# Delta net: the squares of the output norm split into a rounded high part and a low part, summed by rounded products with ones

## The chip, the cores and the metric

The kernel runs on one core of one Trainium2 chip. The metric is the time of one execution on the device, in microseconds (us), as the median of several runs. A core has a matrix engine (TensorE, PE in the profile; its weight loads are PEld), an engine for elementwise work (VectorE, DVE), one for activation functions and copies (ScalarE, ACT), a general one (GpSimd, POOL) and an engine that issues transfers (SyncE, SP). They run side by side, each through its own list of instructions in order, and meet by semaphores. SBUF is the memory that all of them use; TensorE writes only to the eight banks of PSUM.

## The reference, cut to what matters

The program is a stack of layers over 256 tokens with 1024 features: gated feed-forward blocks, an mLSTM mixer, a gated delta net, and attention in a sliding window. All products are of f32 data. The change touches the end of the delta net, the RMS norm of its output over the 128 features of each of 16 heads:

```python
def rmsnorm_2(x, w):
    xf = x.astype(jnp.float32)
    y = xf * lax.rsqrt(jnp.mean(xf * xf, axis=-1, keepdims=True) + EPS)
    return (y * w.astype(jnp.float32)).astype(x.dtype)
...
    o = chunked_gated_delta_rule(q, k, v, g, beta)
    z = z.reshape(bsz, t, GDN_V_HEADS, GDN_HEAD_DIM).astype(jnp.float32)
    o = rmsnorm_2(o, out_norm_w) * jax.nn.silu(z)
    return o.reshape(bsz, t, GDN_V_DIM).astype(hn.dtype) @ w_out
```

## The kernel before, in words

Features lie on the 128 partitions and tokens along the free axis. Every large projection is made of products in a rounded f32 format (`F32R`, fp32r in the profile): a weight tile and an activation are each split into a rounded high part and the rest (`wh`, `wl`, `XH`, `XL`), and three products (high by high, low by high, high by low) are added up in PSUM. ScalarE makes the high parts of the weights (`hi`, L474) and VectorE or GpSimd the low parts (`lo`, L479), from tiles that SyncE brings in through four slots.

The delta net is one large class, `GCore`, in which each engine has its own order written out by hand. A list of step names stands for every engine (`self.A` ScalarE, `self.V` VectorE, `self.T` TensorE, `self.G` GpSimd), and a step's place in its list is the count of a semaphore: `past("sqr0")` waits for the step `sqr0`. Weight products of the projections are set between the steps of the recurrence (`d(h0, h1)` runs quarters of units, each quarter two tiles, that is six products).

The recurrence goes over four groups g = 0 to 3 of four heads, two chunks of 128 tokens each. For a group, TensorE transposes the values of the first chunk (`p1`) and the keys, applies the solved triangle (`p2`), transposes the second chunk (`p1b`), builds the state (`p3`), the first chunk's output (`p3b`), the state's part in the second chunk (`p4`), and the second chunk's values (`p5`) and output (`p6`). VectorE evicts `p1` and `p1b` with a factor (`e1`, L2631; `e1b`, L2645), the keys (`kd`, L2638) and `p4` (`e4`, L2655). ScalarE evicts the others (`e2`, `e3`, `e3b`, `e5` and, last, `e6`, L2263). The output o of a group of heads is then in `dVT`, 128x1024.

The norm is made group by group. `sqr` (ScalarE, L2267) writes the squares of o to `gRO`. `p7` (TensorE, L3277) multiplies them with a 128x128 tile of ones, two f32 products of 512 columns, so that every partition of the two banks holds the sum over the 128 features. `rl` (ScalarE, L2272) takes Ln of the mean, `re` (L2278) Exp of minus half of it. On VectorE `yz` (L2663) multiplies o by the gate, `yo` (L2669) by the norm, and after ScalarE's rounded copy `yh` (L2282) `yl` (L2673) forms the low part `YL`. The output projection `gout0` takes `YH` and `YL`, two of its units to a group; TensorE's unit 4 waits for `yl2`, unit 6 for `yl3`.

The functions that compute this, and the class's list of steps:

Of the kernel before, what the change touches and what calls it, by code (L numbers as in the profile page):

```python
# [23 lines left out]
F32 = mybir.dt.float32  # L24
# [5 lines left out]
P = 128  # L30
# [124 lines left out]
def program(nc, a):  # L155
    with ExitStack() as ctx:
# [1823 lines left out]
        def state_set(n, at, vb_at):  # L1980

            s, = carve(at, 2048, **{f"gS{n}": t4})
            y0, y1 = carve(at + (2176 if n == 0 else 2048), 4096, **{f"gY0_{n}": t4, f"gY1_{n}": t4})
            ro, = carve(at + (2176 if n == 0 else 2048), 4096, **{f"gRO{n}": ([P, HG, SEQ], F32)})
            vb0, vb1, kd = carve(vb_at, 6144, **{f"gVB0_{n}": t4, f"gVB1_{n}": t4, f"gKD{n}": t4})
            return s, y0, y1, ro, vb0, vb1, kd

        sets = [state_set(0, gw, gw + 21504), state_set(1, q0, q0 + 6144), state_set(2, ext + 16384, ext + 16384 + 6144)]
        S0, Y0, Y1, RO, VB0, VB1, KD = ([sets[n][i] for n in (0, 1, 2, 0)] for i in range(7))
        HOP = ((2, 3), (4, 5), (6, 7), (2, 3))  # L1990
        GB = (2, 3, 4, 2)
        KC, EGC, NB, NBC, NC, BW, B2, BR, RK = carve(
# [1 line left out]
            gNBC=([P, GDN_V, 2], F32), gNC=([P, 2, GDN_V], F32), gBW=([P, B], F32), gB2=([P, 2, GDN_V], F32),  # L1994
            gBR=([P, 2, GDN_V], F32), gRK=([P, GDN_V], F32))
        never = cst[:, C_NEVER:C_NEVER + P]
        WS, WS64 = (WS0, WS1), (WL0, WL1)
        BLOCKS = 4
        WP = [bank[2 + i][:, :].rearrange("p (j i) -> p j i", j=16) for i in (0, 1)]
# [5 lines left out]
        class GCore:  # L2005
# [5 lines left out]
            def __init__(self, gate, norm):  # L2011
                self.gate, self.norm = gate, norm
                self.A = steps("act", "gdn_act", (
# [7 lines left out]
                    " re3 yh3").split())  # L2021
                self.V = steps("dve", "gdn_dve", (
# [13 lines left out]
                    " tap43_0 yl0 e4_2 e1_3 kd3 yz1 yo1 yl1 e1b_3 e4_3 yz2 yo2 yz3 yl2 yo3 yl3").split())  # L2036
                self.T = steps("pe", "gdn_pe", (
# [3 lines left out]
                    " p1k_3 p5_2 p7_1 p2_3 p6_2 p1b_3 p3_3 p7_2 p4_3 p3b_3 p5_3 p6_3 p7_3").split())  # L2041
                self.G = steps("pool", "gdn_pool", (
                    "xzero xinit col em1 em0 em2 em3 br nb uzero tzero").split())
                self.s_wd, self.s_w, self.s_xd, self.s_tu = (sem(f"dma_g{n}") for n in ("wd", "w", "xd", "tu"))
                self.units = ([(gqk0, 0, j) for j in range(4)] + [(gk1, 0, j) for j in range(4)]
                              + [(gz1, 0, j) for j in range(4)] + [(gqk1, j // 4, j % 4) for j in range(8)]
                              + [(gz, j // 4, j % 4) for j in range(8)] + [(gv, j // 4, j % 4) for j in range(16)]
                              + [(gout0, 0, j) for j in range(8)] + [(gout1, 0, j) for j in range(4)])
                self.banks = ([4, 5, 6, 7, 1, 2, 3, 0] + [(1, 6, 7, 0)[j % 4] for j in range(8, WIDE)]
                              + [(1, 0)[j % 2] for j in range(WIDE, 44)])  # L2050
# [46 lines left out]
            def act(self, eng):  # L2097
# [166 lines left out]

                def sqr(g):
                    eng.wait_ge(*A.past(f"e6_{g}"))
                    A.done(eng.activation(RO[g][:, :, :], dVT[:, 4 * g:4 * g + 4, :], ACT.Square), f"sqr{g}")  # L2267

                def rl(g):
                    eng.wait_ge(*T.past(f"p7_{g}"))  # L2270
# [209 lines left out]
            def dve(self, eng):  # L2480
# [162 lines left out]
                def e1b(g):  # L2643
                    eng.wait_ge(*T.past(f"p1b_{g}"))
                    V.done(eng.tensor_tensor(VB1[g][:, :, :], quad(bank[HOP[g][0]][:, :], HG), beta(g, 1), ALU.mult),  # L2645
                           f"e1b_{g}")

                def e4(g):
                    eng.wait_ge(*T.past(f"p4_{g}"))
                    r = VB1[g]  # L2650
                    if g == 0:
                        eng.wait_ge(*G.past("nb"))
                    eng.wait_ge(*V.past(f"e1b_{g}"))
                    for h in four:
                        ins = eng.scalar_tensor_tensor(r[:, h, :], bank[HOP[g][1]][:, h * P:(h + 1) * P],  # L2655
                                                       NB[:, 4 * g + h:4 * g + h + 1], r[:, h, :], ALU.mult, ALU.add)
                    V.done(ins, f"e4_{g}")

                def yz(g):
                    o = dVT[:, 4 * g:4 * g + 4, :]  # L2660
                    eng.wait_ge(*A.past(f"sqr{g}"))
                    eng.wait_ge(*A.past(f"zs{g}"))
                    V.done(eng.tensor_tensor(o, o, Z[:, 4 * g:4 * g + 4, :], ALU.mult), f"yz{g}")  # L2663
# [126 lines left out]
                taps(42)  # L2790
                e1b(2)
                e1b(1)
                yz(0)
                yo(0)
                e4(1)
                taps(43)
                yl(0)
                e4(2)
                e1(3)
                kd(3)  # L2800
                yz(1)
                yo(1)
                yl(1)
                e1b(3)
                e4(3)
                yz(2)
                yo(2)
                lo(50)
                yz(3)
                yl(2)  # L2810
                yo(3)
# [240 lines left out]
            def pe(self, eng):  # L3052
# [221 lines left out]
                def p7(g):  # L3274
                    eng.wait_ge(*A.past(f"sqr{g}"))
                    for i in two:
                        mm = eng.matmul(bank[HOP[g][i]][:, :], ones[:, :],  # L3277
                                        RO[g][:, 2 * i:2 * i + 2, :].rearrange("p h t -> p (h t)"), start=True, stop=True)
                    T.done(mm, f"p7_{g}")

                gg()
# [1029 lines left out]
```

## Time and profile before

| | |
|---|---|
| median of 3 runs | 1259.97 us (1258.79 to 1260.63) |
| profiled execution | 1258.97 us, its span 1257.2 us |
| TensorE busy | 1239.2 us, 99% of the span |
| VectorE, ScalarE, GpSimd busy | 888.0, 762.9, 279.2 us (71%, 61%, 22%) |
| mean granted TensorE clock | 0.998 |

The span is the time from the first to the last instruction of the profiled execution. TensorE's busy time counts its matmuls, which overlap in a pipeline: the duration of a matmul in a row is longer than the slot it takes, and the slot is read as the distance from one start to the next. A row of the timeline merges equal instructions that follow each other (x4). "Idle before" in brackets is the time in which the engine had nothing running before the row, and the arrow names what ended it.

### The profile page before, as it was taken

The page shows a single profiled execution, that of the slowest core. Times are in us where ns is not written, and L with a number is a line of the kernel's source. Part 1 is how long each engine was busy: PE and PEld are TensorE (multiplying, and loading weights), DVE is VectorE, ACT ScalarE, POOL GpSimd, SP SyncE. Part 2 cuts the span into 40 slices and gives each one's busy share as a digit, 9 for nine tenths or more (in the row PEclk, how much of TensorE's full clock was granted, in tenths as well). Part 3 has the DMA queues.
Part 4 walks back from the last instruction along what each step waited for, and adds up shares of the span by engine and source line. Part 5 has one row for each costly group of instructions (what it writes and reads, how often), then busy time and mean ns, then how long its engine had stood idle before and what let it go on. Part 6 is the DMA issues. An engine that isn't in the chain of part 4 may idle for free.

```text
span 1257.2 us, 28670 instructions
## 1 busy us (share of the span) xinstructions
PE 1239.2 (99%) x10528; PEld 1213.8 (97%) x10528; DVE 888.0 (71%) x1627; ACT 762.9 (61%) x1284; POOL 279.2 (22%) x240
## 2 busy tenths in 40 slices
PE   9999999999999999999999999999999999999997
PEld 9999999998999999999999989999999989999997
DVE  6766556887787765587796557777766797877654
ACT  6544444598564445468876676666665576766642
POOL 0000000010000000028875320344530131444400
PEclk9999999999999999999999999999999999999999
DMA  7655465464356656646647134865577525665473
GB/s 248 203 170 176 138 173 180 146 193 133 103 175 203 186 155 186 209 131 217 187 155 207 56 102 144 226 196 185 162 204 205 168 69 168 185 190 184 134 205 104
DMA packets 89164, 212.53 MB, mean 169 GB/s; under 512 B 19509, under 2 KB 35701, under 8 KB 88960
## 3 DMA queue, kind: packets, MB, share of 16 engines
q1 hardware_dynamic: 86608, 204.32, 52.6%
q0 software_dynamic: 1632, 6.46, 2.1%
q8 instruction: 49, 0.80, 0.3%
q10 hardware_dynamic: 848, 0.72, 0.2%
q14 instruction: 27, 0.22, 0.1%
HBM read 208.41 MB, written 3.06 MB: 168 GB/s over the span
## 4 chain that ended last, share of the span: by engine, by line
PE 92%; DVE 4%; ACT 2%; issue 1%; DVEq 0%; ACTq 0%
PE bank L624 21%; PE bank L626 21%; PE bank L625 21%; PE bank L3077 3%; PE bank L3078 3%; PE bank L3079 3%; PE bank L1725 1%; PE bank L3212 1%; PE bank L1727 1%; PE bank L1726 1%; DVE wl L479 1%; PE bank L3730 1%; PE bank L3732 1%; PE bank L3731 1%; PE bank L583 1%
## 5 line engine op out<-in xcount | busy, mean ns | idle before, releaser
L474 ACT ACTIVATE wh<-raw 128x1024 fp32r<-128x1024 f32 (+2 forms) x418 | 402.0, 969 | 333.3 <-PE bank L626 288.8
L479 DVE TENSOR_TENSOR wl<-raw,wh 128x1024 fp32r<-128x1024 f32 (+3 forms) x348 | 380.4, 1097 | 139.8 <-ACT wh L474 139.0
L624 PE MATMUL bank<-XH,wh 128*128 128x256 f32 (+1 forms) x1432 | 406.5, 284 | 1.3 <-DVE XL L1064 1.2
L626 PE MATMUL bank<-XH,wl 128*128 128x256 f32 (+1 forms) x1432 | 405.9, 283 | 0.0
L625 PE MATMUL bank<-XL,wh 128*128 128x256 f32 (+1 forms) x1432 | 405.6, 283 | 0.0
L624 PEld LDWEIGHTS bank<-XH,wh 128*128 128x128 f32 x1432 | 270.6, 189 | 2.2 <-DVE XL L1064 1.4
L626 PEld LDWEIGHTS bank<-XH,wl 128*128 128x128 f32 x1432 | 271.0, 189 | 0.0
L625 PEld LDWEIGHTS bank<-XL,wh 128*128 128x128 f32 x1432 | 269.5, 188 | 0.0
L479 POOL TENSOR_TENSOR wl<-raw,wh 128x1024 fp32r<-128x1024 f32 x70 | 168.9, 2421 | 268.0 <-ACT wh L474 267.8
L624 PE MATMUL bank<-AH,wh 128*128 128x256 f32 (+1 forms) x704 | 198.9, 283 | 0.0
L626 PE MATMUL bank<-AH,wl 128*128 128x256 f32 (+1 forms) x704 | 198.7, 282 | 0.0
L625 PE MATMUL bank<-AL,wh 128*128 128x256 f32 (+1 forms) x704 | 198.4, 282 | 0.0
L625 PEld LDWEIGHTS bank<-AL,wh 128*128 128x128 f32 x704 | 132.9, 189 | 0.0
L626 PEld LDWEIGHTS bank<-AH,wl 128*128 128x128 f32 x704 | 132.4, 188 | 0.0
L624 PEld LDWEIGHTS bank<-AH,wh 128*128 128x128 f32 x704 | 132.2, 188 | 0.2
L3077 PE MATMUL bank<-gXH,wh 128*128 128x256 f32 x256 | 75.4, 295 | 0.0
L3078 PE MATMUL bank<-gXL,wh 128*128 128x256 f32 x256 | 71.7, 280 | 0.0
L3079 PE MATMUL bank<-gXH,wl 128*128 128x256 f32 x256 | 71.6, 280 | 0.0
L936 DVE TENSOR_TENSOR tp<-bank,R 128x256 f32<-128x256 f32 x88 | 37.3, 423 | 40.3 <-PE bank L626 33.1
L900 POOL TENSOR_TENSOR AL<-pr,AH 128x256 f32 (+1 forms) x44 | 36.4, 827 | 100.4 <-ACT AH L893 100.2
L948 ACT ACTIVATE bank<-tp,vec 128x256 f32<-128x256 f32 x88 | 48.8, 554 | 3.5 <-DVE tp L936 3.5
L3077 PEld LDWEIGHTS bank<-gXH,wh 128*128 128x128 f32 x256 | 48.2, 188 | 1.4 <-issue 1.0
(401 smaller groups left out, 2274.6 us busy)
## 6 DMA issues: line engine op xcount, KB each, us to landing
raw<-in_w_up SPq DMA_DIRECT2D x170, 512.0 KB, 4.4
raw<-in_w_down SPq DMA_DIRECT2D x64, 384.0 KB, 3.4
raw<-in_w_down SPq DMA_DIRECT2D x64, 320.0 KB, 3.2
raw<-in_w_gvz SPq DMA_DIRECT2D x32, 512.0 KB, 4.5
raw<-in_w_gout SPq DMA_DIRECT2D x16, 512.0 KB, 4.6
raw<-in_w_gqk SPq DMA_DIRECT2D x12, 512.0 KB, 4.0
raw<-in_w_mv SPq DMA_DIRECT2D x8, 512.0 KB, 4.6
raw<-in_w_mqk SPq DMA_DIRECT2D x8, 512.0 KB, 5.0
```

What stands on the lines that cost most here:

```text
L474: eng.activation(WH[s][:, 0:n, :], raw[s][:, 0:n, :], ACT.Copy).then_inc(s_hi[s], 1)
L479: eng.tensor_tensor(WL[s][:, 0:n, :], raw[s][:, 0:n, :], WH[s][:, 0:n, :].bitcast(F32), ALU.subtract).then_inc(s_lo[s], 1)
L583: mm = eng.matmul(bank[st.wide[g]][:, 0:T], WH[u][:, 2 * g + j, :], xl, start=False, stop=k == DC - 1)
L624: eng.matmul(out, WH[s][:, i, :], xh, start=start, stop=False)
L625: eng.matmul(out, WH[s][:, i, :], xl, start=False, stop=False)
L626: mm = eng.matmul(out, WL[s][:, i, :], xh, start=False, stop=stop)
L900: self.lows.done(eng.tensor_tensor(AL[:, bass.ds(j, 1), 0:T], PR[b][:, 0:T].unsqueeze(1), AH[:, bass.ds(j, 1), 0:T].bitcast(F32), ALU.subt ...
L936: leave(st, it, u, eng.tensor_tensor(TP[u % 2][:, 3:3 + T], bank[st.banks[u]][:, 0:T], R[:, 0:T], ALU.mult))
L948: self.tap2s.done(eng.activation(self.sums(u), TP[u % 2][:, 3:3 + T], ACT.Identity, bias=v(self.bias, m), scale=v(self.w, m + 88)), f"tap2 ...
L3077: eng.matmul(out, WH[s][:, i, :], xh, start=first, stop=False)
L3078: eng.matmul(out, WH[s][:, i, :], xl, start=False, stop=False)
L3079: mm = eng.matmul(out, WL[s][:, i, :], xh, start=False, stop=last)
```

## The change

The squares are computed twice. `sqr` on ScalarE now writes them in the rounded format, to a new tile `gROH` that lies over the group's `VB0` and `VB1`. VectorE gets a step `ro`, which forms the same squares in f32 in `gRO`, and `rol`, which takes `gROH` from them and writes the rest, in the rounded format, to `gROL`, in the same place as `gRO`. `p7` then has four products of 512 columns with the same tile of ones, read in the rounded format: two of `gROH`, a wait for `rol`, and two of `gROL` that add to the same banks.

```diff
@@ state_set @@
+            rol, = carve(at + (2176 if n == 0 else 2048), 4096, **{f"gROL{n}": ([P, HG, SEQ], F32R)})
+            roh, = carve(vb_at, 4096, **{f"gROH{n}": ([P, HG, SEQ], F32R)})
+            return s, y0, y1, ro, vb0, vb1, kd, roh, rol
...
+        onesr = ones[:, :].bitcast(F32R)
@@ GCore, ScalarE @@
                 def sqr(g):
                     eng.wait_ge(*A.past(f"e6_{g}"))
-                    A.done(eng.activation(RO[g][:, :, :], dVT[:, 4 * g:4 * g + 4, :], ACT.Square), f"sqr{g}")
+                    A.done(eng.activation(ROH[g][:, :, :], dVT[:, 4 * g:4 * g + 4, :], ACT.Square), f"sqr{g}")
@@ GCore, VectorE @@
+                def ro(g):
+                    o = dVT[:, 4 * g:4 * g + 4, :]
+                    eng.wait_ge(*A.past(f"e6_{g}"))
+                    V.done(eng.tensor_tensor(RO[g][:, :, :], o, o, ALU.mult), f"ro{g}")
+                    eng.wait_ge(*V.past(f"ro{g}"))
+                    eng.wait_ge(*A.past(f"sqr{g}"))
+                    V.done(eng.tensor_tensor(ROL[g][:, :, :], RO[g][:, :, :], ROH[g][:, :, :].bitcast(F32), ALU.subtract),
+                           f"rol{g}")
@@ the order on VectorE @@
                 e1b(1)
+                ro(0)
                 yz(0)
...
                 e4(2)
+                ro(1)
                 e1(3)
...
                 e1b(3)
+                ro(2)
                 e4(3)
                 yz(2)
                 yo(2)
                 lo(50)
+                ro(3)
                 yz(3)
@@ GCore, TensorE @@
                 def p7(g):
                     eng.wait_ge(*A.past(f"sqr{g}"))
                     for i in two:
-                        mm = eng.matmul(bank[HOP[g][i]][:, :], ones[:, :],
-                                        RO[g][:, 2 * i:2 * i + 2, :].rearrange("p h t -> p (h t)"), start=True, stop=True)
+                        eng.matmul(bank[HOP[g][i]][:, :], onesr[:, :],
+                                   ROH[g][:, 2 * i:2 * i + 2, :].rearrange("p h t -> p (h t)"), start=True, stop=False)
+                    eng.wait_ge(*V.past(f"rol{g}"))
+                    for i in two:
+                        mm = eng.matmul(bank[HOP[g][i]][:, :], onesr[:, :],
+                                        ROL[g][:, 2 * i:2 * i + 2, :].rearrange("p h t -> p (h t)"), start=False, stop=True)
                     T.done(mm, f"p7_{g}")
```

The names of the four steps `ro0 rol0` to `ro3 rol3` are set into VectorE's list in the same places. TensorE's and ScalarE's lists stay as they are.

In VectorE's order around group 0, before (`gVB1` is the eviction `e1b`, `dZ` the gate in `yz`, `gNB` the factor in `e4`):

```order
L2645 TENSOR_TENSOR gVB1_2_176<-bank6,gBR_185 128x512 [waits pe_gdn_pe]
L2645 TENSOR_TENSOR gVB1_1_169<-bank4,gBR_185 128x512 [waits pe_gdn_pe]
L2663 TENSOR_TENSOR dVT_97<-dVT_97,dZ_96 128x1024 [waits act_gdn_act]
L2669 SCALAR_TENSOR_TENSOR dVT_97<-dVT_97,vec_62,gRO0_160 128x1024 [waits dve_gdn_dve,act_gdn_act]
L2655 SCALAR_TENSOR_TENSOR gVB1_1_169<-bank5,gNB_180,gVB1_1_169 128x128 [waits dve_gdn_dve,pe_gdn_pe]
```

and with the change:

```order
L2649 TENSOR_TENSOR gVB1_2_180<-bank6,gBR_191 128x512 [waits pe_gdn_pe]
L2649 TENSOR_TENSOR gVB1_1_171<-bank4,gBR_191 128x512 [waits pe_gdn_pe]
L2666 TENSOR_TENSOR gRO0_160<-dVT_97 128x1024 [waits act_gdn_act]
L2669 TENSOR_TENSOR gROL0_164<-gRO0_160,gROH0_165 128x1024 [waits act_gdn_act,dve_gdn_dve]
L2676 TENSOR_TENSOR dVT_97<-dVT_97,dZ_96 128x1024 [waits act_gdn_act]
L2682 SCALAR_TENSOR_TENSOR dVT_97<-dVT_97,vec_62,gRO0_160 128x1024 [waits dve_gdn_dve,act_gdn_act]
L2659 SCALAR_TENSOR_TENSOR gVB1_1_171<-bank5,gNB_186,gVB1_1_171 128x128 [waits dve_gdn_dve,pe_gdn_pe]
```

The two new steps stand behind both evictions and ahead of `yz0`, `yo0` and `e4_1`.

In VectorE's order around groups 2 and 3, with the change (`YL` is `yl1`, then the eviction `e1b_3`; `wl2` is the weight split `lo50`; the last row is `yl2`):

```order
L2686 TENSOR_TENSOR YL_98<-dVT_97,YH_99 128x1024 [waits act_gdn_act]
L2649 TENSOR_TENSOR gVB1_0_162<-bank2,gBR_191 128x512 [waits pe_gdn_pe]
L2666 TENSOR_TENSOR gRO2_178<-dVT_97 128x1024 [waits act_gdn_act]
L2669 TENSOR_TENSOR gROL2_182<-gRO2_178,gROH2_183 128x1024 [waits act_gdn_act,dve_gdn_dve]
L2659 SCALAR_TENSOR_TENSOR gVB1_0_162<-bank3,gNB_186,gVB1_0_162 128x128 [waits dve_gdn_dve,pe_gdn_pe]
...
L479 TENSOR_TENSOR wl2_60<-raw2_52,wh2_56 128x1024 [waits s_hi2]
L2666 TENSOR_TENSOR gRO0_160<-dVT_97 128x1024 [waits act_gdn_act]
L2669 TENSOR_TENSOR gROL0_164<-gRO0_160,gROH0_165 128x1024 [waits act_gdn_act,dve_gdn_dve]
L2676 TENSOR_TENSOR dVT_97<-dVT_97,dZ_96 128x1024 [waits act_gdn_act]
L2686 TENSOR_TENSOR YL_98<-dVT_97,YH_99 128x1024 [waits act_gdn_act]
```

Before, these rows are the same without those of L2666 and L2669: `e4_3` follows `e1b_3`, and `yz3` follows the split.

In TensorE's order at `p7` of group 0, with the change:

```order
L3234 MATMUL bank6<-cst_63,dVT_97 128x128 x3
L3294 MATMUL bank2<-gROH0_165,ones_64 128x512 [waits act_gdn_act]
L3294 MATMUL bank3<-gROH0_165,ones_64 128x512
L3298 MATMUL bank2<-gROL0_164,ones_64 128x512 [waits dve_gdn_dve]
L3298 MATMUL bank3<-gROL0_164,ones_64 128x512
L3272 MATMUL bank5<-gS1_166,dQK_95 128x256 [waits act_gdn_act]
L3272 MATMUL bank5<-gS1_166,dQK_95 128x256
```

Before, two products of `gRO0` stand in the place of the four; the transpose ahead (`p1b` of group 2) and `p4` of group 1 behind are where they were. The wait for VectorE now stands between the second and the third.

## Rows read from the trace of the kernel before

**Rows 1.** The page, busy time by engine and the chain that ended last
```profile
PE 1239.2 (99%) x10528; PEld 1213.8 (97%) x10528; DVE 888.0 (71%) x1627; ACT 762.9 (61%) x1284; POOL 279.2 (22%) x240
...
PE 92%; DVE 4%; ACT 2%; issue 1%; DVEq 0%; ACTq 0%
```

**Rows 2.** Waits of TensorE: us in total, times, longest us
```profile
PE bank L3277 <- ACT gRO L2267: 0.4, 1, 0.4
```

**Rows 3.** Timeline of TensorE, 715 to 754 us: start us, us, what, [idle before]
```profile
715.51 0.60 PE L3217 MATMUL bank<-cst,dVT 128*128 128x128 f32 x4
715.95 1.88 PE L3277 MATMUL bank<-gRO,ones 128*128 128x512 f32 x4
717.67 1.03 PE L3255 MATMUL bank<-gS,dQK 128*128 128x256 f32 x4
...
730.16 1.88 PE L3277 MATMUL bank<-gRO,ones 128*128 128x512 f32 x4
...
739.42 1.88 PE L3277 MATMUL bank<-gRO,ones 128*128 128x512 f32 x4
741.13 1.03 PE L3255 MATMUL bank<-gS,dQK 128*128 128x256 f32 x4
...
751.05 1.99 PE L3277 MATMUL bank<-gRO,ones 128*128 128x512 f32 x4 [0.37 <-ACT gRO L2267]
...
752.99 0.28 PE L3078 MATMUL bank<-YL,wh 128*128 128x256 f32 x1
753.11 0.28 PE L3079 MATMUL bank<-YH,wl 128*128 128x256 f32 x1
```

**Rows 4.** Timeline of VectorE, 716 to 750 us
```profile
716.15 1.29 DVE L2645 TENSOR_TENSOR gVB<-bank,gBR 128x512 f32<-128x512 f32 x2
717.36 1.22 DVE L2663 TENSOR_TENSOR dVT<-dVT,dZ 128x1024 f32<-128x1024 f32 x1
720.26 1.28 DVE L2669 SCALAR_TENSOR_TENSOR dVT<-dVT,vec,gRO 128x1024 f32<-128x1024 f32 x1 [1.68 <-ACT gRO L2278]
...
728.28 0.69 DVE L2631 TENSOR_TENSOR gVB<-bank,gBR 128x512 f32<-128x512 f32 x1 [1.45 <-PE bank L3217]
...
738.83 1.23 DVE L2673 TENSOR_TENSOR YL<-dVT,YH 128x1024 fp32r<-128x1024 f32 x1 [3.09 <-ACT YH L2282]
...
748.67 1.22 DVE L479 TENSOR_TENSOR wl<-raw,wh 128x1024 fp32r<-128x1024 f32 x1 [2.71 <-ACT wh L474]
```

**Rows 5.** Timeline of VectorE near 635 us, steps that wait for each other
```profile
635.41 0.43 DVE L2598 TENSOR_TENSOR bank<-bank,gX 128x256 f32<-128x256 f32 x1
635.87 0.42 DVE L2602 TENSOR_TENSOR gX<-gX,bank 128x256 f32<-128x256 f32 x1
```

**Rows 6.** Timeline of ScalarE, 727 to 750 us
```profile
727.27 0.58 ACT L2263 ACTIVATE dVT<-bank 128x512 f32<-128x512 f32 x1
...
728.22 1.06 ACT L2267 ACTIVATE gRO<-dVT 128x1024 f32<-128x1024 f32 x1
...
736.16 0.60 ACT L2263 ACTIVATE dVT<-bank 128x512 f32<-128x512 f32 x1 [1.19 <-PE bank L3270]
736.79 1.06 ACT L2267 ACTIVATE gRO<-dVT 128x1024 f32<-128x1024 f32 x1
737.76 1.04 ACT L2282 ACTIVATE YH<-dVT 128x1024 fp32r<-128x1024 f32 x1
...
749.30 0.60 ACT L2263 ACTIVATE dVT<-bank 128x512 f32<-128x512 f32 x1 [0.67 <-PE bank L3270]
749.94 1.06 ACT L2267 ACTIVATE gRO<-dVT 128x1024 f32<-128x1024 f32 x1
```

**Rows 7.** Busy time in windows at the end: us, each engine (x), PEclk, DMA
```profile
1251.00:1251.50 0.50, 0.23 (x3) 0.00 (x0) 0.45 (x2) 0.23 (x1) 0.00 (x0) 1.00 0.00 0
1252.00:1252.50 0.50, 0.00 (x0) 0.00 (x0) 0.50 (x2) 0.00 (x0) 0.50 (x2) 0.50 0.00 0
```

**Rows 8.** Timeline of TensorE, at the start and at the end
```profile
1.89 5.59 PE L632 MATMUL bank<-ones,mean 128*128 128x128 f32 x30 [1.89 <-DVE rel L4144]
...
1250.85 0.38 PE L4205 MATMUL bank<-cst,RC 128*128 128x128 f32 x2
```

More of the change, by code:

```diff
@@ L1985, in state_set @@
             vb0, vb1, kd = carve(vb_at, 6144, **{f"gVB0_{n}": t4, f"gVB1_{n}": t4, f"gKD{n}": t4})
-            return s, y0, y1, ro, vb0, vb1, kd
+            rol, = carve(at + (2176 if n == 0 else 2048), 4096, **{f"gROL{n}": ([P, HG, SEQ], F32R)})
+            roh, = carve(vb_at, 4096, **{f"gROH{n}": ([P, HG, SEQ], F32R)})
+            return s, y0, y1, ro, vb0, vb1, kd, roh, rol
         sets = [state_set(0, gw, gw + 21504), state_set(1, q0, q0 + 6144), state_set(2, ext + 16384, ext + 16384 + 6144)]
-        S0, Y0, Y1, RO, VB0, VB1, KD = ([sets[n][i] for n in (0, 1, 2, 0)] for i in range(7))
+        S0, Y0, Y1, RO, VB0, VB1, KD, ROH, ROL = ([sets[n][i] for n in (0, 1, 2, 0)] for i in range(9))
         HOP = ((2, 3), (4, 5), (6, 7), (2, 3))
@@ L2034, in __init__ @@
                     " c2_2 tap39_2 tap39_1 tap39_0 c6_1 c2_3 e1b_0 kd0 tap40_2 tap40_1 tap40_0 c6_2 c6_3 e4_0 tap41_2"
[1 row of a table removed]
-                    " tap43_0 yl0 e4_2 e1_3 kd3 yz1 yo1 yl1 e1b_3 e4_3 yz2 yo2 yz3 yl2 yo3 yl3").split())
[2 rows of a table added]
+                    " yo3 yl3").split())
                 self.T = steps("pe", "gdn_pe", (
```

3 rows, old and new, of the table WP are left out of this document.

## The prediction, made before the changed kernel ran

> **What bounds the kernel now.** I read the page's busy shares and its chain first. TensorE is busy 99% of the span and holds 92% of the chain [rows 1]. So a microsecond of work less on TensorE is a microsecond less of span, and a microsecond in which it waits is one more, unless work after it takes that back. Next, the waits by engine, TensorE alone: of the 18 us of the span in which it is not busy, the product that the change rewrites (L3277) waited 0.4 us, once in its four calls; the other three found their operand ready [rows 2]. Then the timeline of the three engines around those four calls, 715 to 760 us. The reader is to see in it that TensorE has no gap there, that VectorE and ScalarE have several, and that all three walk through lists of a fixed order, so a late item holds back all behind it. I call the four groups of heads group 0 to 3.
>
> **What TensorE saves.** Each call of `p7` is two f32 products over 512 columns, which the trace shows as 4 records. From its start at 715.95 to the next product's at 717.67 is 1.72 us, 0.43 a record; group 2 (739.42 to 741.13) gives the same [rows 3]. The change issues 4 products of 512 columns in the rounded format. None of that size is in the trace. The nearest row is the rounded product over 256 columns, which takes a slot of 0.118 us (752.99 to 753.11) [rows 3]. At the same rate per column 512 columns are 0.225 us (0.236 as two whole slots); the other end is 0.43, what a record of the f32 product over as many columns takes. I take 0.225, since the slot of the format itself is the nearest row: a call is then 0.90 us, and 4 x (1.72 - 0.90) = 3.3 us are saved if nobody waits. At 0.43 nothing is saved.
>
> The Trainium skill (TensorE: Matmul & The Clock Gate, Back-to-back issue gap) gives a sustained spacing of about 131 ns for 512 columns in a stream of weight loads and matmuls. By it a call would take 0.52 us, and, as only the second half of a call counts where the engine waits, my sum would come out some 0.8 us lower. The trace speaks against it: at 256 columns the slot is already 118 ns, and I keep the slot that scales with the columns.
>
> **What is added.** VectorE gets two operations of 128x1024 f32 a group: the square (`ro`) and the square less its rounded part (`rol`). Operations of that size with both inputs in SBUF take 1.22 us there, with an f32 result (717.36) and with a rounded one (738.83) [rows 4]; `rol` also waits for `ro`, and such a step that waits for the one just before it on VectorE starts 0.03 us after that one's end (635.41 + 0.43 to 635.87) [rows 5]. So `ro` and `rol` together hold VectorE for 1.22 + 0.04 + 1.22 = 2.48 us, 9.9 us in the four groups. ScalarE's square keeps its size and place and only writes another tile in the rounded format; its conversion to that format at the same size (L2282) takes 1.04 where the square takes 1.06 [rows 6], so I put it at nothing. The wait on `rol` stands in the middle of `p7`, after two of the four products. Behind it on TensorE stand the recurrence of the next group (`p4`) and the projections. So what counts is when `rol` is ready, group by group.
>
> **Group 0.** TensorE comes to `p7` at 715.95, and nothing ahead of that changes. VectorE is then at `e1b_2` and `e1b_1`, which end at 716.15 + 1.29 = 717.44, the next operation starting at 717.36 [rows 4]. `ro0` has that start in the changed order, and `rol0` ends at 717.36 + 2.48 = 719.84. TensorE has done its first two products by 715.95 + 0.45 = 716.40 and stands until 719.90 (0.06 for the hand-over, as 749.94 + 1.06 to 751.05 shows [rows 3, 6]): 3.50 us. It ends the call at 720.35, not 717.67: +2.68. The Ln, the Exp and the final product of this group come from `p7`, as do TensorE's next steps and their evictions; they all move by the same 2.68. From here I keep the times of before and count on top of that shift.
>
> **Group 1.** The eviction `e6_1` ends at 727.27 + 0.58 = 727.85 [rows 6], and VectorE is free by then: the row of its next step, at 728.28, has 1.45 us of idle time before it [rows 4]; the square on ScalarE ends at 728.22 + 1.06 = 729.28 [rows 6]. `ro1` ends at 729.10, `rol1` at 730.54, when TensorE, at 730.16 + 0.45 = 730.61, asks for it. No wait; 0.82 saved. `e1_3`, queued behind `rol1`, becomes ready near 731.2 where it was 729.0, and TensorE wants it only after `p7` and 12 more products, at 732.5.
>
> **Group 2.** TensorE, now 0.82 earlier, comes to `p7` at 739.42 - 0.82 = 738.60 and is through the first half at 739.05. VectorE must first do `yl1` and `e1b_3`. `yl1` waits for the copy `yh1` on ScalarE, which stands behind `e6_2` and `sqr2`, and those follow TensorE: `e6_2` at 736.16, which waited 1.19 us for it, and `yh1` at 737.76 [rows 6] become 735.34 and 736.94, with `sqr2` between them. So `yl1` starts at 738.01 (before: 738.83), `e1b_3` at 739.15, and `ro2` at 739.75, as two evictions of this size take 717.36 - 716.15 = 1.21 us up to the next start, 0.60 each [rows 4]. `rol2` ends at 742.23, TensorE goes on at 742.29: a wait of 3.24 us. The call ends at 742.74, not 741.13: +1.61.
>
> **Group 3.** VectorE has the split `lo50` at 748.67 + 1.61 = 750.28, done at 751.50 [rows 4]; `e6_3` ends then too (749.30 + 0.60 + 1.61 [rows 6]). `ro3` starts at 751.54 and `rol3` ends at 754.02. TensorE starts the call at 751.05 + 1.61 = 752.66, is half way at 753.11, waits until 754.08 (0.97) and ends at 754.53, where before it was at 752.99 - 0.12 = 752.87: +1.66. Last, `yl2` is now queued behind `ro3`, `rol3` and `yz3`: it ends near 756.30. The fifth unit of the output projection wants it 11 slots after 752.99, at 754.28, so now at 755.94; a wait of 0.43. `yl3` has over a microsecond to spare.
>
> **Sum.** Waits 3.50 + 0 + 3.24 + 0.97 + 0.43 = 8.1; saved 3.3; net +4.8 us (by the shifts: 2.68 + 1.66 + 0.43). After 760 us TensorE is busy without a stop, and the waits that remain there are for work that its own results start, so I see nothing that takes it back. GpSimd's splits run beside some of these operations, but VectorE's 1.22 stayed the same in all of them. The profiled execution took 1258.97 us (span 1257.2), so 1263.8 by its time; the median of the runs shown is 1.0 above it, so I forecast 1264.8. With a price of 0.43 the second half costs 0.86 behind each wait, group 1 saves nothing, and the same walk gives +6.5.
>
> **The rivals.**
> (1) The clock falls in a wait. The granted clock is 1.00 in the window from 1251.0 and 0.50, the 1.2 GHz level, in the one from 1252.0 [rows 7]; TensorE had its last products, small ones, from 1250.85 [rows 8], so it fell soon after they ended. Two full stops of over 3 us are near enough to that to matter; against it, here the engine is dense on either side. The price from the slower level: the 30 records at the start took 5.59 us [rows 8] where records of that shape take 0.11 (715.51 to 715.95 for 4) [rows 3], so 2.3 us lost for a cold stretch. One fall gives 1267.1, two 1269.4. The Trainium skill (TensorE: Matmul & The Clock Gate, Part 1) says that the slow clock is the default and activity releases it; by that rule, the trace agrees at the end of the program, and a long stop may count as idle. Chance 22%.
> (2) Rounded products cost as much per column as f32 ones over 512 columns: 1266.5. For it: no row of this size. Against: the 0.118 slot. 6%.
> (3) Faster: `rol` is ready when TensorE asks, the 3.3 us are gained, 1256.7. Place: group 0 and group 2. It decides where the waits add up to less than 3.3. For it: VectorE is idle 1.7 us before `yo0` (720.26) and 3.1 us before `yl1` (738.83) [rows 4]. Against: that idle time lies behind `ro` and `rol` in the order or ahead of work that TensorE's own pace sets, and 2.48 us of work cannot be done in the 0.45 us that the first half lasts, with VectorE 1.4 us late already. 4%.
> (4) No change: the delay is taken back later, or it covers other waits: 1260. Nothing in the waits speaks for it. 5%.
>
> **Numbers.** My forecast has 63%. The range should hold it and one fall of the clock: 1262.6 (a microsecond of run and of each estimate below) to 1267.8. What can be told from no change here is 0.2%, 2.5 us: forecast, (1) and (2) are slower by more, 91% together less 2% for a forecast that comes out under 2.5; (4) and those 2% are same, 7%; faster 4%.
>
> **What would show it.** After: waits of TensorE on `gROL` at the four calls of about 3.5, 0, 3.2 and 1.0 us, and 0.4 on `YL`; rounded 512-column products in slots near 0.22; eight added VectorE operations of 1.22; clock 1.00 through 700 to 760. If the waits of groups 0 and 2 are under 1.5 us each the forecast is wrong, and the step that failed is the place of `ro` in VectorE's order; if the slots are 0.43, it is the price.

## The result, and the profile after

The change makes the kernel slower: 1270.79 us (median of 6 runs, 1268.76 to 1272.72) against 1259.83 us, a ratio of 1.0091 (95% interval 1.0081 to 1.0101). That is 11.0 us more, where 4.8 were forecast, and 3.0 us above the upper end of the range (1267.8). The profiled execution took 1270.91 us, its span is 1269.1.

These are the busy times and the chain on the page of the changed kernel, to be held against [rows 1]:

```profile
PE 1242.3 (98%) x10528; PEld 1217.8 (96%) x10528; DVE 898.4 (71%) x1635; ACT 763.2 (60%) x1284; POOL 280.2 (22%) x240
...
PE 90%; DVE 5%; ACT 2%; issue 1%; DVEq 0%; ACTq 0%
```

TensorE has less work to do and is still busy 3.1 us longer, and there are 8.8 us more in which it isn't busy. Its waits in the changed kernel (L3298 is the second half of `p7`, L3094 the output projection; total, times, longest) say where these are:

```profile
PE bank L3298 <- DVE gROL L2669: 8.6, 3, 4.6
PE bank L3294 <- ACT gROH L2271: 0.4, 1, 0.4
PE bank L3094 <- DVE YL L2686: 0.2, 1, 0.2
```

The timeline of TensorE in the changed kernel at the calls of groups 0, 1, 2 and 3 (columns as in [rows 3]; L3294 is the first half of `p7`, L3234 the transpose ahead, L3229 the products that were L3212 before, L3095 and L3096 products of a projection):

```profile
716.14 0.60 PE L3234 MATMUL bank<-cst,dVT 128*128 128x128 f32 x4
716.50 0.71 PE L3294 MATMUL bank<-gROH,ones 128*128 128x512 f32 x2
720.51 0.91 PE L3298 MATMUL bank<-gROL,ones 128*128 128x512 f32 x2 [3.31 <-DVE gROL L2669]
...
723.78 0.41 PE L3095 MATMUL bank<-gXL,wh 128*128 128x256 f32 x1
723.99 0.41 PE L3096 MATMUL bank<-gXH,wl 128*128 128x256 f32 x1
...
725.16 1.06 PE L3229 MATMUL bank<-gY,gKD 128*128 128x128 f32 x8
...
735.17 0.63 PE L3294 MATMUL bank<-gROH,ones 128*128 128x512 f32 x2
735.68 0.74 PE L3298 MATMUL bank<-gROL,ones 128*128 128x512 f32 x2
...
737.67 1.05 PE L3229 MATMUL bank<-gVB,gU 128*128 128x128 f32 x8
...
743.79 0.63 PE L3294 MATMUL bank<-gROH,ones 128*128 128x512 f32 x2
749.04 1.22 PE L3298 MATMUL bank<-gROL,ones 128*128 128x512 f32 x2 [4.62 <-DVE gROL L2669]
...
756.30 1.05 PE L3229 MATMUL bank<-gVB,gU 128*128 128x128 f32 x8
...
762.34 0.73 PE L3294 MATMUL bank<-gROH,ones 128*128 128x512 f32 x2 [0.37 <-ACT gROH L2271]
763.76 0.73 PE L3298 MATMUL bank<-gROL,ones 128*128 128x512 f32 x2 [0.70 <-DVE gROL L2669]
...
764.45 0.28 PE L3095 MATMUL bank<-YL,wh 128*128 128x256 f32 x1
```

The reader is to see two things. The waits of the four calls are 3.3, 0, 4.6 and 0.7 us. And behind the two long ones the engine is slow for a while: a rounded product of 256 columns takes a slot of 0.21 us (723.78 to 723.99), where [rows 3] have 0.12. The windows of the changed kernel show why (us; busy time of PE, PEld, DVE, ACT, POOL; then the granted clock):

```profile
717.50:720.50 3.00, 0.00 (x0) 0.00 (x0) 2.97 (x4) 0.00 (x0) 0.36 (x1) 1.00 0.38 124
721.50:724.00 2.50, 2.50 (x10) 2.12 (x10) 0.25 (x2) 2.28 (x3) 0.00 (x0) 0.50 0.00 0
724.50:727.50 3.00, 3.00 (x29) 3.00 (x28) 1.67 (x5) 1.08 (x2) 0.00 (x0) 1.00 0.00 0
744.50:747.50 3.00, 0.00 (x0) 0.00 (x0) 3.00 (x2) 0.12 (x1) 2.14 (x1) 1.00 0.05 18
748.50:751.50 3.00, 2.46 (x6) 1.99 (x7) 0.49 (x1) 1.20 (x2) 0.00 (x0) 0.50 0.40 141
751.50:754.50 3.00, 3.00 (x15) 2.91 (x14) 2.26 (x5) 0.85 (x3) 0.00 (x0) 0.50 0.00 0
755.50:758.50 3.00, 3.00 (x29) 3.00 (x28) 1.07 (x1) 1.30 (x2) 2.22 (x1) 1.00 0.00 0
```

TensorE does nothing from 717.5 to 720.5. In the window from 721.5 the granted clock is 0.50, the 1.2 GHz level, and from 724.5 it is 1.00 again. (The numbers of matmuls in these windows can't be compared, since their shapes differ; the slot of one shape can, 0.21 against 0.12 us.) The same comes with the wait of group 2, and lasts longer: 0.50 in both windows from 748.5 to 754.5.

There is a third cause, on VectorE. These are its timeline and GpSimd's in group 2 of the changed kernel (L2686 is `yl1`, L2649 `e1b_3`, L2666 and L2669 `ro2` and `rol2`, L479 on GpSimd the split `lo48`):

```profile
743.22 1.23 DVE L2686 TENSOR_TENSOR YL<-dVT,YH 128x1024 fp32r<-128x1024 f32 x1 [2.50 <-ACT YH L2286]
744.36 0.68 DVE L2649 TENSOR_TENSOR gVB<-bank,gBR 128x512 f32<-128x512 f32 x1
744.96 2.77 DVE L2666 TENSOR_TENSOR gRO<-dVT 128x1024 f32<-128x1024 f32 x1
747.76 1.23 DVE L2669 TENSOR_TENSOR gROL<-gRO,gROH 128x1024 fp32r<-128x1024 f32 x1
```
```profile
744.21 2.43 POOL L479 TENSOR_TENSOR wl<-raw,wh 128x1024 fp32r<-128x1024 f32 x1 [6.33 <-ACT wh L474]
```

`ro2` takes 2.77 us, not 1.22. Counted back by 1.22 from its end, it would have begun at 746.5, when the split that began ahead of it was ending (744.21 + 2.43 = 746.64).

**The ledger** is made from how far a row of the changed kernel lies behind the same one of before. Ahead of `p7` of group 0 it is 0.63 us (716.14 against 715.51 [rows 3]). That is a late start of this execution: its first 30 products took 6.28 us, where [rows 8] have 5.59. The rows of before that the ledger uses and [rows 3] do not show are these:

```profile
720.13 1.06 PE L3212 MATMUL bank<-gY,gKD 128*128 128x128 f32 x8
...
733.29 1.05 PE L3212 MATMUL bank<-gVB,gU 128*128 128x128 f32 x8
...
745.01 1.05 PE L3212 MATMUL bank<-gVB,gU 128*128 128x128 f32 x8
```

With a half call of 0.45 us behind each wait:

| place | how far behind | step | forecast |
|---|---|---|---|
| end of `p7`, group 0 | 720.51 + 0.45 against 717.67: 3.29 | +2.66 | +2.68 |
| slow clock after it | 725.16 against 720.13: 5.03 | +1.74 | 0 |
| `p7`, group 1 | 737.67 against 733.29: 4.38 | -0.65 | -0.82 |
| end of `p7`, group 2 | 749.04 + 0.45 against 741.13: 8.36 | +3.98 | +2.43 |
| slow clock after it | 756.30 against 745.01: 11.29 | +2.93 | 0 |
| `p7`, group 3 | 764.45 against 752.99: 11.46 | +0.17 | +0.05 |
| wait for `YL` | 0.2 | +0.2 | +0.43 |

The steps add up to 11.0, as much as the medians differ. The two traces themselves end 11.3 us apart beyond the late start (last product at 1262.78 against 1250.85), so 0.3 us lie outside the ledger. Of the 11.0, 4.7 is the slow clock, 1.55 of group 2's step is `ro2` beside the split, and what is left is 4.8, the sum that was forecast.

### The profile page after: what moved, and what is told of

The parts are those of the page before. It is cut to its first block, busy times and chain, and to the rows that moved or that the text cites. A ratio compares the mean times of both kernels' runs of the same rounds, so it can differ in the third digit from the quotient of the medians.

```text
span 1269.1 us, 28682 instructions
## 1 busy us (share of the span) xinstructions
PE 1242.3 (98%) x10528; PEld 1217.8 (96%) x10528; DVE 898.4 (71%) x1635; ACT 763.2 (60%) x1284; POOL 280.2 (22%) x240
## 3 DMA queue, kind: packets, MB, share of 16 engines
HBM read 208.41 MB, written 3.06 MB: 167 GB/s over the span
## 4 chain that ended last, share of the span: by engine, by line
PE 90%; DVE 5%; ACT 2%; issue 1%; DVEq 0%; ACTq 0%
PE bank L624 21%; PE bank L626 20%; PE bank L625 20%; PE bank L3094 3%; PE bank L3095 3%; PE bank L3096 3%; PE bank L1725 1%; PE bank L1727 1%; PE bank L1726 1%; PE bank L3229 1%; DVE wl L479 1%; PE bank L3751 1%; PE bank L3753 1%; PE bank L3752 1%; PE bank L583 1%
## 5 line engine op out<-in xcount | busy, mean ns | idle before, releaser
L479 DVE TENSOR_TENSOR wl<-raw,wh 128x1024 fp32r<-128x1024 f32 (+3 forms) x348 | 381.3, 1100 | 139.3 <-ACT wh L474 138.6
L479 POOL TENSOR_TENSOR wl<-raw,wh 128x1024 fp32r<-128x1024 f32 x70 | 168.2, 2410 | 278.3 <-ACT wh L474 278.2
L3094 PE MATMUL bank<-gXH,wh 128*128 128x256 f32 x256 | 75.8, 296 | 0.0
L3095 PE MATMUL bank<-gXL,wh 128*128 128x256 f32 x256 | 71.9, 281 | 0.0
L3096 PE MATMUL bank<-gXH,wl 128*128 128x256 f32 x256 | 71.7, 280 | 0.0
L3094 PEld LDWEIGHTS bank<-gXH,wh 128*128 128x128 f32 x256 | 48.4, 189 | 1.4 <-issue 1.0
```

Of the source, the lines that this page charges most:

```text
L479: eng.tensor_tensor(WL[s][:, 0:n, :], raw[s][:, 0:n, :], WH[s][:, 0:n, :].bitcast(F32), ALU.subtract).then_inc(s_lo[s], 1)
L3094: eng.matmul(out, WH[s][:, i, :], xh, start=first, stop=False)
L3095: eng.matmul(out, WH[s][:, i, :], xl, start=False, stop=False)
L3096: mm = eng.matmul(out, WL[s][:, i, :], xh, start=False, stop=last)
```

## The experiments

My theory after the traces has three causes: the waits of the sum (4.8), two falls of the clock at the long waits (4.7), and `ro2` held up by GpSimd's split (1.5). The rivals are that the slow clock costs nothing of its own, and that `ro2` was slow for another reason.

**TensorE kept at work in the waits.** Products that are then overwritten are set ahead of the two products of the high part in `p7`:

```diff
+                    for i in two * (7, 0, 10, 0)[g]:
+                        eng.matmul(bank[HOP[g][i]][:, :], onesr[:, :],
+                                   ROH[g][:, 2 * i:2 * i + 2, :].rearrange("p h t -> p (h t)"), start=True, stop=True)
```

> The change, with the first two products of p7 (rounded high part, 512 columns) repeated 7 times in group 0 and 10 times in group 2, each repeat overwriting the bank; the results are the same and TensorE works through the waits for rol. At 0.23 us a product that is 3.2 us and 4.6 us of filler inside waits that were 3.3 and 4.6 us. Theory (the waits, plus two falls of TensorE's clock behind them): the granted clock stays 1.00 through 700 to 770 us and 1.7 + 3.0 us come back: 1266.1. Rival (the slow clock costs nothing beyond the waits, the rest of the loss is elsewhere): 1270.8, unchanged.

Measured: 1266.06 us, ratio 1.0054 (1.0040 to 1.0068). In its trace the clock stands at 1.00 over the whole stretch, and the waits for `rol` are down to one of 0.7 us:

```profile
715.00:760.00 45.00, 43.87 (x311) 39.64 (x310) 33.27 (x43) 28.87 (x38) 10.15 (x5) 1.00 0.27 88
```
```profile
716.17 3.50 PE L3294 MATMUL bank<-gROH,ones 128*128 128x512 f32 x14
...
720.19 0.73 PE L3301 MATMUL bank<-gROL,ones 128*128 128x512 f32 x2
```

Work of no use, put where TensorE would stand, takes 4.2 us off the loss (11.0 to 6.8 against the kernel before). The rival is out: the slow clock is a cost of its own.

**The split `lo48` on VectorE**, behind `rol2`:

```diff
@@ VectorE @@
                 ro(2)
+                lo(48)
                 e4(3)
@@ GpSimd @@
                 lo(47)
-                lo(48)
                 lo(49)
```

> The change, with the weight split lo48 taken from GpSimd and done on VectorE behind rol of group 2. Theory (GpSimd's split and the square ro of group 2 need the same port of SBUF, so ro2 stood 1.55 us): ro2 takes 1.22 us instead of 2.77, the wait of group 2 falls from 4.6 to 3.1 us, 1.5 us come back, and with the shorter wait the clock falls for one period or not at all behind group 2 (1.7 to 3.0 us more): 1266.3 to 1269.3. Rival (ro2 was slow for another reason, such as a read of a tile still being written): ro2 stays 2.8 us and the time 1270.8.

Measured: 1268.49 us, ratio 1.0072 (1.0058 to 1.0086). `ro2` takes 1.22 us, and the wait of group 2 is 3.1 us. Its VectorE and TensorE:

```profile
745.21 1.22 DVE L2666 TENSOR_TENSOR gRO<-dVT 128x1024 f32<-128x1024 f32 x1
746.47 1.23 DVE L2669 TENSOR_TENSOR gROL<-gRO,gROH 128x1024 fp32r<-128x1024 f32 x1
```
```profile
747.75 0.94 PE L3298 MATMUL bank<-gROL,ones 128*128 128x512 f32 x2 [3.06 <-DVE gROL L2669]
```
```profile
748.50:751.00 2.50, 2.50 (x9) 2.14 (x8) 0.89 (x4) 1.26 (x2) 0.00 (x0) 0.50 0.41 108
752.00:755.00 3.00, 3.00 (x29) 3.00 (x28) 1.98 (x2) 2.55 (x4) 0.52 (x1) 1.00 0.02 8
```

So the split on GpSimd was what held `ro2`. The clock falls at a wait of 3.1 us too, but it is back at 1.00 by 752, where in the changed kernel it was still 0.50 to 754.5. Behind group 2 the slow clock then costs 1.7 us, not 2.9 (the row 745.01 of before is at 753.77 here). By the traces the edit brings back 2.8 us (1.55 and 1.2), by the medians 1.8, with an interval as wide as 1.8 us to either side.

**Both edits** (with 7 repeats in groups 0 and 2):

> Both edits: lo48 on VectorE behind rol of group 2, and the first products of p7 repeated 7 times in groups 0 and 2. Theory: neither the clock nor the port costs anything, only the waits of the prediction's sum are left: 1264.7. If a fourth cause is at work the time stays above 1266.

Measured: 1264.81 us, ratio 1.0045 (1.0031 to 1.0059), 5.5 us above the kernel before in the same set of runs (1259.29). That is the forecast's sum of 4.8 and 0.7 more, within the interval (3.9 to 7.4), which would also leave room for another cause of up to 2.6 us.

**The rounded products alone**, with `ro`, `rol` and the wait left out, and the high part taken again in place of the low part:

```diff
                     for i in two:
                         eng.matmul(bank[HOP[g][i]][:, :], onesr[:, :],
                                    ROH[g][:, 2 * i:2 * i + 2, :].rearrange("p h t -> p (h t)"), start=True, stop=False)
-                    eng.wait_ge(*V.past(f"rol{g}"))
                     for i in two:
                         mm = eng.matmul(bank[HOP[g][i]][:, :], onesr[:, :],
-                                        ROL[g][:, 2 * i:2 * i + 2, :].rearrange("p h t -> p (h t)"), start=False, stop=True)
+                                        ROH[g][:, 2 * i:2 * i + 2, :].rearrange("p h t -> p (h t)"), start=False, stop=True)
```

> The change without VectorE's part: ro and rol are left out, p7 has its four rounded products of 512 columns but all of the high part (the second two take the high part in place of the low one, so the sum is doubled), and waits only for sqr. It measures the price of the rounded products alone. Theory (0.22 to 0.23 us a slot where an f32 product took 0.86): 4 x 0.8 = 3.2 us below the kernel before, 1256.7. Rival (rounded products of 512 columns cost as much per column as f32 ones): 1259.8, no change.

Measured: 1255.90 us, ratio 0.9974 (0.9964 to 0.9983): 3.4 us faster, where 3.2 were expected. In its trace the four products of group 2 take 0.93 us in all, 0.23 each, to the start of `p4` (L3268):

```profile
738.23 0.62 PE L3290 MATMUL bank<-gROH,ones 128*128 128x512 f32 x2
738.69 0.63 PE L3293 MATMUL bank<-gROH,ones 128*128 128x512 f32 x2
739.16 1.08 PE L3268 MATMUL bank<-gS,dQK 128*128 128x256 f32 x4
```

**Both orders made for the change.** VectorE takes `ro` and `rol` of groups 0 and 2 as soon as the group's output exists, TensorE puts `p4` of group 1 ahead of `p7` of group 0, and group 3, where I saw nothing that could hide `rol`, stays in f32:

```diff
@@ VectorE @@
-                taps(42)
+                ro(0)
                 e1b(2)
                 e1b(1)
-                ro(0)
+                e4(1)
                 yz(0)
                 yo(0)
-                e4(1)
+                taps(42)
                 taps(43)
...
+                ro(2)
                 yl(1)
                 e1b(3)
-                ro(2)
...
-                ro(3)
@@ TensorE @@
-                p7(0)
                 p4(1)
+                p7(0)
```

> The change in groups 0 to 2 with both orders made for it, group 3 left in f32 as before. VectorE: ro0 and rol0 ahead of e1b_2, e1b_1, e4_1, yz0 and yo0, with the taps of unit 42 behind these; ro2 and rol2 ahead of yl1 and e1b_3. TensorE: p4 of group 1 ahead of p7 of group 0. Theory (the loss is only a matter of when rol is ready; the clock follows the waits): rol0 ends 0.1 us before TensorE asks and rol2 at about the time, no wait over 0.3 us, the clock stays 1.00, ro2 runs ahead of GpSimd's lo48; three calls save 0.8 us each, less 0.2 for p4: 2.2 us below the kernel before, 1257.4. Rival (VectorE's 7.4 us of added work push something else late, whatever the order): 1259.5 or more.

Measured: 1258.49 us, ratio 0.9999 (0.9990 to 1.0008). It gets the whole loss back, but of the 2.2 us that were expected nothing can be told from no change. The wait of group 2 is gone, and one of 1.6 us is left in group 0. Behind that one the clock stays at 1.00. VectorE in its trace:

```profile
713.96 1.65 DVE L2666 TENSOR_TENSOR gRO<-dVT 128x1024 f32<-128x1024 f32 x1 [3.54 <-ACT dVT L2267]
715.64 3.27 DVE L2669 TENSOR_TENSOR gROL<-gRO,gROH 128x1024 fp32r<-128x1024 f32 x1
```

I had moved `ro0` and `rol0` into the middle of four splits in a row on GpSimd, and looked only at VectorE for room. They took 1.65 and 3.27 us, as `ro2` had taken 2.77.

**One quarter of the projection ahead of `p7` of group 3**, in that kernel and, as a control, in the kernel before:

```diff
-                d(188, 190)
+                d(188, 191)
                 p7(3)
-                d(190, 208)
+                d(191, 208)
```

> The same, with one quarter (six products) of the output projection moved ahead of p7 of group 3, where TensorE stood 0.5 us for the square. Theory: that wait goes too, and yl3 still comes in time for its unit: 2.7 us below the kernel before, 1256.9. Rival (the later p7 makes yl3 late by as much): as without it, 1257.4.

> The kernel before with only that quarter moved ahead of p7 of group 3, the control for the run above. Theory: 0.4 us below the kernel before, 1259.2, at the edge of what five rounds can tell. Rival: no difference.

Measured: 1258.35 us, ratio 0.9997 (0.9988 to 1.0006), and 1258.39 us, ratio 0.9995 (0.9986 to 1.0004). The theories were 2.7 and 0.4 us below the kernel before. Both traces have no wait for the square of group 3 any more, but neither time can be told from no change; whether the 0.4 us came back stays open.

**A split less on GpSimd.** This is the reordered kernel with the moved quarter, and with `lo46`, which TensorE needs only much later, done by VectorE ahead of `ro1`:

```diff
@@ VectorE @@
                 e4(2)
+                lo(46)
                 ro(1)
@@ GpSimd @@
                 lo(44)
-                lo(46)
                 lo(47)
```

> The reordered kernel with the moved quarter (f2), and the weight split lo46 taken from GpSimd and done on VectorE ahead of ro1. In f2 TensorE still waited 1.6 us for rol0, since ro0 took 1.65 and rol0 3.27 us beside four splits in a row on GpSimd. Theory (the port of SBUF): GpSimd is through 2.4 us sooner, ro0 takes at most 1.9 us and rol0 1.22, the wait for rol0 is under 0.3 us, and 1.4 to 1.6 us come back against f2: 1256.9, some 2.1 us below the kernel before. Rival (something else holds rol0, or lo46 on VectorE makes another step late): 1258.4, as f2.

Measured: 1257.51 us, ratio 0.9987 (0.9978 to 0.9996) to the kernel before, 1258.82 in that set. `ro0` still runs into the third split and takes 1.65 us, but `rol0` takes its 1.22:

```profile
714.54 1.65 DVE L2666 TENSOR_TENSOR gRO<-dVT 128x1024 f32<-128x1024 f32 x1 [3.53 <-ACT dVT L2267]
716.23 1.23 DVE L2669 TENSOR_TENSOR gROL<-gRO,gROH 128x1024 fp32r<-128x1024 f32 x1
```

TensorE doesn't wait in group 0 any more. The one wait for `gROL` that is left is a new one, in group 1:

```profile
727.34 1.22 DVE L479 TENSOR_TENSOR wl<-raw,wh 128x1024 fp32r<-128x1024 f32 x1
728.48 1.22 DVE L2666 TENSOR_TENSOR gRO<-dVT 128x1024 f32<-128x1024 f32 x1
```
```profile
731.01 0.73 PE L3303 MATMUL bank<-gROL,ones 128*128 128x512 f32 x2 [0.51 <-DVE gROL L2669]
```

So both the theory and a part of its rival came true. The 1.6 us of group 0 are gone, and `lo46`, which now stands ahead of `ro1` on VectorE, makes `rol1` late by 0.5 us. This version is 1.3 us faster than the kernel before, where 2.1 were expected. What it gains over the kernel without this edit is not shown: that one was 0.7 us ahead of the kernel before in its own set of runs, this one is 1.3 ahead in another, and the difference of 0.6 us is smaller than the uncertainty of either (1.1 us). The same holds against the control with the moved quarter alone, also 0.7 us ahead.

## Why the prediction was wrong

The direction was right, and so was the part of the mechanism that the sum holds. The waits of the four calls were forecast as 3.50, 0, 3.24 and 0.97 us and came as 3.3, 0, 4.6 and 0.7; the slot of a rounded product of 512 columns as 0.225, measured 0.23; the saving without waits as 3.3, measured 3.4. The sum of these terms, 4.8 us, is what the ledger has when the two other causes are taken out, and what the kernel with both edits shows within its interval. That it fits to a tenth is luck in part: group 1 saved 0.65 us, not 0.82, and the wait for `YL` was 0.2, not 0.43. Two steps failed.

The first and larger one is that the sum has no term for the slow clock: it takes TensorE's rate behind a wait to be the rate ahead of it. The runs showed 4.7 us in its place, 1.7 behind group 0 and 2.9 behind group 2. The fall of the clock was written down as rival (1), for which the rows spoke [rows 7, 8], but it had 22%, and the range was cut behind a single fall. What I set against it, that "the engine is dense on either side", protected nothing here: the clock fell at a stop of 3.3 us with TensorE busy all the time up to it, and so it did at those of 4.6 and 3.1 us. The rival's price for two falls, 1269.4, came within 1.4 us of the result. Its 2.3 us a fall happens to be the mean of two different ones, and what it lacks is the term of the next paragraph. The forecast also treated the two falls as chances, though both waits were nearly the same length, so that whatever held for one was likely to hold for the other.

The second is the sentence that "VectorE's 1.22 stayed the same in all of them", by which `ro2` has 1.22 us in the sum. It took 2.77, so 1.55 us are missing there. The sentence was read from rows in which the case did not arise. In that stage of the trace of before, none of the steps that ran beside a split both read two tiles in SBUF and began after it: the evictions read one operand from PSUM, and `yz1` (729.55), `yl1` (738.83) and `yo2` (744.67) began ahead of the split. Earlier in the same trace the case is there. A step of 128x256 on two tiles in SBUF that began after a split took 2.18 us, where the next one, at 661.16, took 0.43:

```profile
659.05 2.18 DVE L2578 TENSOR_TENSOR dQK<-dQK,gEG 128x256 f32<-128x256 f32 x1
```
```profile
658.57 2.38 POOL L479 TENSOR_TENSOR wl<-raw,wh 128x1024 fp32r<-128x1024 f32 x1 [0.43 <-ACT wh L474]
```

It ended at 661.23, and the split at 660.95. `yz1` at 729.55 shows the same from the other side. In the trace of before, on GpSimd:

```profile
730.30 2.70 POOL L479 TENSOR_TENSOR wl<-raw,wh 128x1024 fp32r<-128x1024 f32 x1 [13.11 <-ACT wh L474]
```

This split began while `yz1` ran and took 2.70 us, where the median of the 70 splits is 2.40: here GpSimd was the one to stand. The Trainium skill (SBUF — State Buffer, Who interferes with whom) states just this: a VectorE instruction with two SBUF inputs and a GpSimd instruction that reads SBUF exclude each other, and the later one stands until the first is through. The traces agree (2.77 and 3.27 us for steps of 1.22). The forecast should have laid GpSimd's splits beside every new step; `ro2` was to start at 739.75 and `lo48` began at 739.83 in the trace of before, so the forecast's own times put them side by side. In the changed kernel the split was the first, by 0.75 us. `yz1` was held there too (2.16 us, beside the split of 735.33), at no cost, as `yo1` then still waited 0.47 us for the Exp.

The two failures feed each other: the split made the wait of group 2 longer, and with the longer wait the clock stayed down for longer (2.9 us lost, against 1.7 with `lo48` on VectorE). Rivals (2), (3) and (4) are out: the slot of a rounded product is 0.23 us, `rol` was late in three of four groups, and nothing took the delay back after 760 us.

## What to carry to other kernels

In this kernel, where TensorE is packed, a wait of three microseconds or more in its middle cost the wait and then the slow clock with it, 1.7 to 2.9 us a time. Give such a case the larger chance, and put other work, even useless work, into the wait. Where a step is added on VectorE that reads two tiles from SBUF, look at what GpSimd does at that moment, and not only at VectorE's idle time; and where a step is moved to VectorE, look at what it makes late there. A cheaper product pays only if what feeds it is ready: four calls were worth 3.4 us here with nothing to wait for. With the two steps at the places of the change the kernel lost 11 us, and with the orders of VectorE, TensorE and GpSimd changed around them, and group 3 left as it was, it gained 1.3.

## What the runs showed of the hardware that was not expected

The first point is how short a stop was enough. TensorE stood for 3.06 us in the kernel with `lo48` on VectorE, after a dense stretch, and the clock fell to 0.50. At the stop of 1.59 us in the first reordered kernel it stayed at 1.00. No trace here has a stop in a busy stretch whose length lies between these two.

In the profiled executions of two kernels (the rounded products alone, and the first one with new orders) the clock was also slow for a while near 342 us, in a part that no edit touches. The same window of the kernel before and of the reordered one:

```profile
336.00:344.00 8.00, 6.33 (x51) 5.79 (x50) 6.33 (x14) 4.01 (x9) 0.00 (x0) 1.00 0.43 131
```
```profile
336.00:344.00 8.00, 6.64 (x43) 6.00 (x42) 6.33 (x15) 4.01 (x9) 0.00 (x0) 0.79 0.40 130
```

TensorE is busy 6.3 of 8.0 us there in the kernel before, so it has idle time in which slower products fit. The slow clock cost nothing that shows: the reordered kernel was 0.35 us ahead of the one before at 336 us (336.14 against 336.49 for the same product) and 0.34 at 712. At the waits of `p7`, with packed work behind them, the same clock cost 1.7 and 2.9 us.
